# Encoder layer: high parts of the gated projection given places of their own, all eight weight groups split in one go, taps in fourteen score steps

## The reference

```
xn   = RMSNorm(x)
proj = xn @ w_in + b_in                    -> glu_a, glu_g, q, k, v  (512 columns each)
conv = silu(LayerNorm(depthwise_conv31(glu_a * sigmoid(glu_g))))
attn = neighbourhood attention of q, k, v  (8 heads, 4 column blocks of 128 tokens)
h    = x + [conv; attn] @ w_out + b_out
h    = h + top-4-of-32 experts (clamped SwiGLU) of RMSNorm(h)
out  = RMSNorm(h)
```

## Time and profile before

| | |
|---|---|
| runs, median of 3 (lowest to highest) | 1338.12 us (1337.47 to 1338.19) |
| the profiled execution's own time | 1338.11 us |
| its span in the trace | 1336.3 us |
| TensorE busy | 1269.6 us, 95% of the span |
| VectorE busy | 1227.8 us, 92% |
| ScalarE busy | 972.3 us, 73% |
| TensorE's granted clock, mean over the span | 0.983 of full speed |

### The profile page before, as it was taken

How to read it: one execution, slowest core, us unless ns; L and a number is a source line. 1 busy time by engine, 2 the same in 40 slices (tenths; PEclk the granted TensorE clock), 3 DMA queues, 4 the chain that set the end, 5 groups by cost and what they waited for, 6 DMA issues and landing times.

```text
span 1336.3 us, 17611 instructions
## 1 busy us (share of the span) xinstructions
PE 1269.6 (95%) x5771; PEld 1011.6 (76%) x5771; DVE 1227.8 (92%) x1010; ACT 972.3 (73%) x788; POOL 182.7 (14%) x181
## 2 busy tenths in 40 slices
PE   4999889789999999999999999999999999999996
PEld 4887668667878778787777777878777777777775
DVE  6799956699999999999999999999999999999997
ACT  4241664448797978788888888797979787878762
POOL 5001000112010101010110102020101010101252
PEclk9999889889999999999999999999999999999999
DMA  9945401499999999999999999999999999999984
GB/s 284 389 170 142 157 1 52 150 365 400 397 401 422 409 421 409 419 410 421 409 420 409 417 410 422 408 418 414 409 419 411 422 409 418 407 419 421 408 319 157
DMA packets 83974, 473.31 MB, mean 354 GB/s; under 512 B 10059, under 2 KB 10358, under 8 KB 34790
## 3 DMA queue, kind: packets, MB, share of 16 engines
q1 hardware_dynamic: 71726, 436.57, 81.1%
q0 software_dynamic: 7072, 19.39, 4.6%
q10 hardware_dynamic: 5144, 16.93, 3.4%
HBM read 447.72 MB, written 29.33 MB: 357 GB/s over the span
## 4 chain that ended last, share of the span: by engine, by line
PE 69%; DVE 15%; DMA 6%; ACT 5%; issue 3%; ACTq 1%; SPq 0%; POOL 0%; DVEq 0%
PE pair L1936 14%; PE pair L1937 13%; PE pair L1938 13%; PE pair L1952 6%; PE pair L1953 6%; DMA w_raw<-in_w_up 6%; DVE w_low L1283 5%; DVE area_m L1134 4%; ACT w_high L833 2%; PE pair L1923 2%; PE pair L1971 2%; PE pair L1950 1%; PE pair L1714 1%; PE pair L1715 1%; PE pair L1716 1%
## 5 line engine op out<-in xcount | busy, mean ns | idle before, releaser
L1283 DVE TENSOR_TENSOR w_low<-w_raw,w_high 128x2048 fp32r<-128x2048 f32 x380 | 838.2, 2245 | 41.3 <-ACT w_high L833 40.0
L833 ACT CAST w_high<-w_raw 128x2048 fp32r<-128x2048 f32 x380 | 703.0, 1878 | 170.5 <-PE pair L1938 117.5
L1936 PE MATMUL pair<-w_high,xT_high 128*128 128x512 f32 x528 | 211.2, 400 | 0.0
L1937 PE MATMUL pair<-w_low,xT_high 128*128 128x512 f32 x528 | 206.6, 391 | 0.0
L1938 PE MATMUL pair<-w_high,xT_low 128*128 128x512 f32 x528 | 206.0, 390 | 0.0
L1952 PE MATMUL pair<-w_high,xS 128*128 128x512 f32 x450 | 183.3, 407 | 0.1
L1953 PE MATMUL pair<-w_low,xS 128*128 128x512 f32 x450 | 175.7, 390 | 0.0
L1936 PEld LDWEIGHTS pair<-w_high,xT_high 128*128 128x128 f32 x528 | 99.1, 188 | 31.9 <-issue 11.4
L1938 PEld LDWEIGHTS pair<-w_high,xT_low 128*128 128x128 f32 x528 | 99.2, 188 | 21.6
L1937 PEld LDWEIGHTS pair<-w_low,xT_high 128*128 128x128 f32 x528 | 99.2, 188 | 19.2
L1936 PE MATMUL pair<-w_high,hT_high 128*128 128x512 f32 x256 | 102.1, 399 | 11.1 <-DVE w_low L1283 11.1
(11 more groups left out here) (355 smaller groups left out, 1800.5 us busy)
## 6 DMA issues: line engine op xcount, KB each, us to landing
w_raw<-in_w_gate SPq DMA_DIRECT2D x128, 1024.0 KB, 15.5
w_raw<-in_w_up SPq DMA_DIRECT2D x128, 1024.0 KB, 16.9
w_raw<-in_w_down SPq DMA_DIRECT2D x128, 1024.0 KB, 16.8
ring<-in_w_in SPq DMA_DIRECT2D x5, 2048.0 KB, 18.7
y_rows<-area_t SPq DMA_DIRECT2D x1, 8704.0 KB
y_rows<-area_m ACTq DMA_DIRECT2D x15, 512.0 KB
ring<-in_w_out SPq DMA_DIRECT2D x2, 2048.0 KB, 7.9
y_rows<-area_t SPq DMA_DIRECT2D x1, 3840.0 KB, 38.6
```

The source lines that it names most:

```text
L833: s.copy(w_high[:, i % HIGH_RING, raw:], w_raw[i][:, raw:]).then_inc(high_ready, 1)
L1283: v.tensor_tensor(w_low[i][:, raw:], w_raw[i][:, raw:], w_high[:, i % HIGH_RING, raw:].bitcast(F32), ALU.subtract).then_inc(low_ready, 1)
L1936: t.matmul(to[half], tok_high, hi, start=(opens and kk == 0), stop=False)
L1937: t.matmul(to[half], tok_high, lo, start=False, stop=False)
```

## The change

The high parts of groups 4 to 7 get places of their own, 1024 words each, in `area_q` and `area_k`. Until then these areas hold the normalised tokens that TensorE transposes and the row of norm weights, so the first of them waits for the end of the transposes and of the normalisation, and no group waits for TensorE's earlier groups. All eight groups are split ahead of the first gate product, the four of unit 1 first, then the four of unit 2; TensorE's order stays, and its waits count by the new order of splits. The taps behind the first and the second gate product go from 9 and 10 to 12 and 13, and `TAP_STEPS` from 18 to 14.

```diff
+        glu_next = [over(f"glu_next{i}", (q_at, k_at)[i // 2], 1024 * (i % 2), [P, KD, P]) for i in range(4)]
...
+        split_order = (0, 2, 4, 6, 1, 3, 5, 7) + tuple(range(8, 20))
+        split_place = [split_order.index(g) for g in range(20)]
...
-            high = glu_high[:, g % 4] if g < 8 else q0_high[:, :, :] if g == 8 else (q_high, k_high)[place - 3][:, c]
+            high = glu_high[:, g] if g < 4 else glu_next[g - 4][:, :, :] if g < 8 else q0_high[:, :, :] if g == 8 else (q_high, k_high)[place - 3][:, c]
...
-        TAP_STEPS = 18
+        TAP_STEPS = 14
...
-                if 4 <= g < 8:
-                    act.wait_ge(proj_done, g - 3)
+                if g == 4:
+                    act.wait_ge(xn_transposed, 2 * NQ)
+                    act.wait_ge(xn_ready, NQ)
...
-            for g in range(4):
+            for g in split_order[0:8]:
                 win_high_part(g)
...
-                for g in {0: (4, 5), 1: (6, 7, 8)}.get(c, ()):
-                    win_high_part(g)
+                if c == 1:
+                    win_high_part(8)
...
-                dve.wait_ge(win_high_ready, g + 1)
+                dve.wait_ge(win_high_ready, split_place[g] + 1)
...
-            for g in range(4):
+            for g in split_order[0:8]:
                 win_low_part(g)
             dve.wait_ge(upad_zeroed, 1)
             glu(0)
-            win_low_part(4)
-            win_low_part(5)
-            taps(9, known=1)
+            taps(12, known=1)
             glu(1)
-            win_low_part(6)
-            win_low_part(7)
-            taps(10, known=2)
+            taps(13, known=2)
             glu(2)
...
-                pe.wait_ge(win_low_dve, g + 1)
+                pe.wait_ge(win_low_dve, split_place[g] + 1)
```

## The result

| | before | with the change |
|---|---|---|
| median of 5 runs (lowest to highest) | 1337.47 us (1336.2 to 1338.19) | 1343.91 us (1339.83 to 1345.76) |
| ratio, 95% interval | | 1.0046 (1.0035 to 1.0057) |
| the profiled execution's own time | 1338.11 us | 1339.83 us |

The change makes the kernel slower by 0.46%, with an interval wholly above 0.2%. The forecast was 1339.0, in a range up to 1341.1.

A forecast was written before the change was run, and what follows sets the result against it. VectorE was taken to bound the loop up to the score of i = 14, TensorE from 165.22 us on. +1.33 + 0.36 - 0.48 - 0.3 = +0.9 us on 1338.12 gave 1339.0 us, range 1336.2 to 1341.1.

The forecast's parts named there:

- Part 1 and 2: Projections: ScalarE's casts hidden by 5.32 us of idle time; VectorE's early splits end at 34.3, first gate product unmoved.
- Part 3: Behind the first two gate products: six taps made early at no cost, TensorE setting both times, no microsecond won yet.
- Part 4: VectorE's run ahead of the first score: 21 taps become 23, costing 2 x 0.66 = 1.33 us; first score at 137.4.
- Part 5: Attention loop: one channel alone in steps 8 to 13, 0.12 us more each; steps 8 to 10 cost 0.36 us.
- Part 6: Steps without taps: 0.48 us of TensorE idle time goes, product 1.2 us late; the low clock's end leaves 0.6 to 1.2.
- the first rival: TensorE's low clock of 164 to 171 us does not come back: 1336.9 us, at most down to 1335.2; chance 0.20.
- The third rival: Steps 18 to 20, behind the mean products: low clock lasts one 3.4 us stretch longer, +2.9 us, 1341.0; chance 0.11.
- The signs: Profile marks: splits by 34.3, first score 137.4, VectorE waiting over 8 us in steps 14 to 18, i = 18 transposes 176.4.

The follow-up runs named there:

- e1: Changed kernel with 18 tap steps instead of 14, so 15 taps ahead of the first score: 1336.82 us, ratio 0.9998 to the kernel before.
- e7: Changed kernel with 15 tap steps instead of 14, so 21 taps ahead of the first score: 1337.54 us, ratio 1.0007 to the kernel before.
- e5: The changed kernel itself measured once more, beside the later runs on one chip: 1344.71 us, ratio 1.0061 to the kernel before.
- e4: Changed kernel with ten unused 128x512 products on TensorE between the last v product and step 0: 1337.33 us, ratio 1.0006 to the kernel before.
- e10: Changed kernel with TensorE's wait for the last v copy moved behind step 0, and 16 tap steps: 1338.71 us, ratio 1.0006 to the kernel before.
- e11: e10 with each tap from the fiftieth on choosing among three unfinished channels instead of two: 1337.06 us, ratio 1.0007 to the kernel before.
- e14: Single execution of the unaltered changed kernel, made for its trace: 1344.13 us.
- e13: Single execution of the unaltered changed kernel, made for its trace: 1340.03 us.
- e2: Kernel before with 14 tap steps instead of 18 and nothing else, so 29 taps ahead of the first score: 1350.29 us, ratio 1.0091.
- e6: Kernel before with two more unused ScalarE copies ahead of the last v copy, lengthening TensorE's gap: 1343.84 us, ratio 1.0057.
- e3: Changed kernel with ScalarE's copy of the last v block ahead of the third exponential: 1339.29 us, ratio 1.0014 to the kernel before.
- e8: e1 with an unused 128x192 float32 product on TensorE in each of steps 2 to 9: 1337.33 us, ratio 1.0003 to the kernel before.
- e9: Changed kernel with TensorE's wait for the last v copy moved behind step 0, ahead of the first v product: 1339.83 us, ratio 1.0021.

## Why the prediction was wrong

**Part 1 and 2, high and low parts at no cost: right.** All splits were done at 34.04, the first gate product waited for TensorE as before, and e1, which has just these and the moved early taps, stands at 0.9998.

**Part 3, six taps early, nothing won yet: right**, and it stayed so to the end. The text left open what becomes of VectorE's time when the loop's start is not VectorE's. e1 shows it: 2.36 us of waiting.

**Part 4, two late taps at 1.33 us: the step that failed.** The length was right, by VectorE's own account. The sentence "VectorE has no idle time between the fourth gate product and the first score, so this costs 2 x 0.66" stops at VectorE. The scores release the exponentials, the third exponential stands on ScalarE ahead of the last copy of v, and TensorE awaits that copy with an idle time of 1.15 us already there. The prediction says nothing of TensorE between its last v product and step 0, and its rows of TensorE begin at 164 us. In place of 1.33 us the two taps cost some 6 us (1343.91 - 1337.47 = 6.4 for the whole change, 7.2 between e7 and e5). How it divides is an estimate: the gap grew by 1.2 us, and e4, which keeps the late start and fills the gap, lost only 0.8; the other 5 or so are the low clock behind it.

**Part 5, 0.12 us for each step with one channel: right in size** (1.79 us in e10, 1.67 in e11), and its place on the path is not shown: the forecast took three such steps as 0.36 us of delay, while e11 got hardly 0.1 us of four of them through to `attn_low`. The Trainium skill, "VectorE: DVE Perf Modes", section "The DRAIN you can't avoid", measures for copies in a row that a semaphore between two costs nothing extra; for a tap that reads the result of the one just before it, e10 and e11 measure 0.12 us for two taps' step.

**Part 6, the clock: wrong in its place.** It took the low stretches of one execution as fixed, and asked only how the delay of 1.69 us would meet them. They move from execution to execution. The argument against the first rival, that the runs shown lie within 0.72 us, rested on three runs; in the 86 runs of the kernel before that stand beside the experiments it lies between 1334.91 and 1340.87 us.

**The third rival** had the right kind, a low clock that lasts longer, and the wrong place: it put it in steps 18 to 20, one stretch of 3.4 us long, at 1341.0. In e14 it lasted from step 0 to about 177 us. The price can be read off the transposes: those of step 0 came 0.92 us later than in the trace of before (142.53 against 141.61), those of i = 14 7.0 us (171.07 against 164.06), those of i = 18 6.3 us. So all of the loss behind the gap lies in the steps up to 14; 0.7 us of it come back by i = 18.

**The signs** named for the changed kernel were mostly there in its profile, and the time was still wrong. Two were missed: VectorE waited 1.16 + 5.49 = 6.65 us in steps 14 to 18, not over 8, and the transposes of i = 18 stood at 175.25 instead of 176.4. The first score came before 137, which was named as a sign of being wrong, but only because the whole execution ran 0.8 us early. None of the signs looks at TensorE's idle time ahead of step 0.

That the profiled execution lies so near the forecast (1339.83 against 1339.0) is luck. With the 0.8 us of the earlier start its delay at i = 18 is 0.5 us; another 2.0 us were lost behind that point, where the low stretch at 190 us was longer, and no part of the sum has them.

**Still open.** Why the clock rises again at about 145 us in some executions with the longer gap and stays down for 30 us in others, with TensorE as busy in both, isn't settled. The Trainium skill, "TensorE: Matmul & The Clock Gate", section "What's actually happening", says that the monitor behind this clock runs free and does not start anew with the kernel. That would let the same gap count in one execution and not in another, as e13 and e14 show; no run here tests it by itself. The same section has activity release the low clock; from 142.90 to 160 us in e14 TensorE was busy without a gap, with small products, and it was not released.

## What to carry to other kernels

When work is moved ahead of a point on one engine, follow its results through the other engines' queues to the engine that sets the end, and ask there how long it already stands idle: an idle stretch of TensorE ahead of a run of small products has two prices, its length and the clock behind it, and here the second was several times the first (about 5 us against 1, an estimate). Time gained on an engine ahead of a stage that another engine starts is worth nothing (e1), and time lost there may cost more than itself (e2, e6). Where a kernel is near such an edge, one profile is one draw: look at several executions, and let filler work or an undone part (e4, e7) tell what the clock costs.

## What the runs showed of the hardware

- Behind an idle time of 2.12 to 2.37 us on TensorE, in place of 1.15, the granted clock fell from 1.00 to 0.50 in four of six traces, each time 0.1 to 0.4 us behind the start of the first transposes (read from the clock of stretches of 1 us); in the traces with 1.15 us (before, e1, e3, e7, e8) and with 1.46 us (e9) it was 1.00 from 140 to 145 us. The ratios go the same way: 1.0057 and 1.0061 (2.12 and 2.35 us), 1.0021 (1.46 us), 0.9998 to 1.0014 (1.15 us, or filled). Single executions of e1, e3 and e7 at 1342.8 us or more, with mean clocks of 0.975 to 0.977, show that 1.15 us doesn't rule out a low clock for longer; where it stood in them isn't known, as they have no trace.
- Once low, the clock can stay low for over 30 us while TensorE is 97% busy: 29.01 of 30.00 us in e14 from 145 to 175 us, all at 0.50. The products there have 64 to 256 columns, but for the first of the mean's (512), from 173.85 us on.
- Ten products of 128x512 in the gap (2.43 us at full clock) stood in place of the idle time in e4, and the clock was 1.00 from 140 to 150 us in its trace.
